# Both seams around an MLP: weight splits in other places, gating on VectorE alone, and a product that goes through its input tiles outside its banks

## The reference, cut to what matters

```python
x = x + m[2] * rms_norm(y, g_post_mix)                       # seam 1: y is the attention's output
f = channel_mlp(modulate(x, g_pre_mlp, m[3], m[4]), w_in, w_out)
x = x + m[5] * rms_norm(f, g_post_mlp)                       # seam 2
# then the next block: modulate(x, g_pre_mix, ...) and its projections
```

## Time and profile before

| | us |
|---|---|
| median of 3 runs | 2458.89 (2457.56 to 2459.14) |
| the profiled execution | 2459.46 |
| its span in the trace | 2458.1 |
| PE busy | 2296.6 (93%) |
| PEld busy | 2095.1 (85%) |
| DVE busy | 1218.8 (50%) |
| ACT busy | 969.9 (39%) |
| POOL busy | 508.9 (21%) |
| DMA, mean over the span | 140 GB/s |

### The profile page before, as it was taken

How to read it: one execution, slowest core, us unless ns; L and a number is a source line. 1 busy time by engine, 2 the same in 40 slices (tenths; PEclk the granted TensorE clock), 3 DMA queues, 4 the chain that set the end, 5 groups by cost and what they waited for, 6 DMA issues and landing times.

```text
span 2458.1 us, 37770 instructions
## 1 busy us (share of the span) xinstructions
PE 2296.6 (93%) x16663; PEld 2095.1 (85%) x16663; DVE 1218.8 (50%) x1517; ACT 969.9 (39%) x1153; POOL 508.9 (21%) x453
## 2 busy tenths in 40 slices
PE   6999899989999999899999899979999979888998
PEld 6999889869999999568999777867888868667997
DVE  5645566556546544456555456352223264544434
ACT  3433444444434333344443345333322334444442
POOL 2112344412112111221220110011211310220220
PEclk8999999999999999799999999989999989899999
DMA  6554443455555554796545110122323323113551
GB/s 246 172 178 166 140 136 123 133 191 172 180 181 177 183 180 157 261 309 239 185 168 187 53 35 18 43 95 86 103 93 96 103 81 103 52 52 103 187 178 64
DMA packets 205246, 344.72 MB, mean 140 GB/s; under 512 B 8846, under 2 KB 69499, under 8 KB 205083
## 3 DMA queue, kind: packets, MB, share of 16 engines
q1 hardware_dynamic: 205082, 342.31, 41.7%
HBM read 341.24 MB, written 1.05 MB: 139 GB/s over the span
## 4 chain that ended last, share of the span: by engine, by line
PE 80%; DVE 9%; POOL 5%; ACT 4%; issue 2%; SPq 0%; DMA 0%; DVEq 0%; POOLq 0%; ACTq 0%
PE PS L467 77%; PE PS L476 3%; DVE WL L453 2%; ACT WH L440 1%; POOL small L1504 1%; DVE rstd L588 1%; DVE XL L635 1%; POOL TMP L1513 1%; POOL small L1502 1%; DVE TMP L1430 0%; DVE XL L1003 0%; DVE al L999 0%; POOL TMP L1514 0%; DVE small L1408 0%; DVE TMP L1435 0%
## 5 line engine op out<-in xcount | busy, mean ns | idle before, releaser
L453 DVE TENSOR_TENSOR WL<-raw,WH 128x2048 fp32r<-128x2048 f32 (+2 forms) x281 | 651.5, 2330 | 721.0 <-ACT WH L440 721.0
L467 PE MATMUL PS<-XH,WH 128*128 128x256 f32 (+1 forms) x2336 | 700.3, 300 | 40.9 <-issue 15.3
L467 PE MATMUL PS<-XL,WH 128*128 128x256 f32 (+1 forms) x2336 | 693.8, 297 | 0.0
L467 PE MATMUL PS<-XH,WL 128*128 128x256 f32 (+1 forms) x2336 | 693.5, 297 | 0.0
L440 ACT ACTIVATE WH<-raw 128x2048 fp32r<-128x2048 f32 (+2 forms) x281 | 518.9, 1859 | 361.5 <-PE PS L467 361.0
L467 PEld LDWEIGHTS PS<-XH,WH 128*128 128x128 f32 x2336 | 452.5, 194 | 57.0 <-issue 18.5
L467 PEld LDWEIGHTS PS<-XL,WH 128*128 128x128 f32 x2336 | 453.5, 194 | 10.0
L467 PEld LDWEIGHTS PS<-XH,WL 128*128 128x128 f32 x2336 | 453.1, 194 | 10.0
L467 PE MATMUL PS<-WH,XH 128*128 128x256 f32 (+2 forms) x944 | 288.3, 305 | 19.1 <-DVE XL L635 8.1
L467 PE MATMUL PS<-WL,XH 128*128 128x256 f32 (+2 forms) x944 | 279.6, 296 | 0.0
L467 PE MATMUL PS<-WH,XL 128*128 128x256 f32 (+2 forms) x944 | 279.4, 296 | 0.0
(11 more groups left out here) (236 smaller groups left out, 2556.8 us busy)
## 6 DMA issues: line engine op xcount, KB each, us to landing
raw<-in_ffn_w_in SPq DMA_DIRECT2D x88, 1024.0 KB, 5.1
raw<-in_w_mod SPq DMA_DIRECT2D x48, 1024.0 KB, 5.3
raw<-in_ffn_w_out SPq DMA_DIRECT2D x40, 1024.0 KB, 4.9
raw<-in_a_w_in SPq DMA_DIRECT2D x36, 1024.0 KB, 4.9
raw<-in_w_mlp_in SPq DMA_DIRECT2D x32, 1024.0 KB, 5.5
raw<-in_w_mlp_out SPq DMA_DIRECT2D x32, 1024.0 KB, 5.0
raw<-in_gla_w_in SPq DMA_DIRECT2D x12, 1024.0 KB, 5.0
raw<-in_attn_w_qkv SPq DMA_DIRECT2D x6, 1024.0 KB, 5.1
```

Source lines behind the costliest of these rows:

```text
L453: dve.e.tensor_tensor(self.WL[j % NRAW][:, 0:nk * nn], self.raw[j % NRAW][:, 0:nk * nn], wh.bitcast(F32), ALU.subtract).then_inc(*self.lo. ...
L467: return self.pe.e.matmul(out, l, r, start=start, stop=stop, skip_group_check=skip)
```

## The change

- The bodies of the split loops become `act_part` and `dve_part`, each of which splits one chunk.
- In the seams, ACT splits the next product's first chunk behind the root of "y1" and its second behind the squares of "n1", ahead of that norm's root. Before, both splits stood behind that root. The copy or square of `Y`'s second half for h=0 goes behind the root.
- DVE splits the first chunk behind the gating of h=1 and the second one a place later, both ahead of the reciprocal of "n1" as before, but no longer waiting for ACT's splits behind the root. The modulation's bias moves into the prenorm, behind the step k = 5.
- All four gatings are on DVE; `gated_pool`, `rest_pool` and the signal `res_pool` go. The third chunk's split on DVE goes behind the gating of h=0.
- `pe_halves` takes the input tiles as the outer loop and the banks as the inner one, and its hooks are called once for each h.

```diff
     def act_begin(self, n=1, held=0):
-        act = self.act
         for i in range(n):
             self.act_begun += 1
             while self.act_split < len(self.parted) and self.parted[self.act_split] < self.act_begun + AHEAD - (held if i + 1 == n else 0):
-                q = self.act_split
-                j = self.parted[q]
-                _, nk, nn, _ = self.stream[j]
-                act.wait_ge(self.raws[j % NRAW], j)
-                if q >= NW:
-                    act.wait_ge(self.lin, self.parted[q - NW])
-                act.e.activation(self.WH[q % NW][:, 0:nk * nn], self.raw[j % NRAW][:, 0:nk * nn], ACT.Copy).then_inc(*self.hi.up(j))
-                self.act_split += 1
+                self.act_part()
+
+    def act_part(self):
+
+        act, q = self.act, self.act_split
+        j = self.parted[q]
+        _, nk, nn, _ = self.stream[j]
+        act.wait_ge(self.raws[j % NRAW], j)
+        if q >= NW:
+            act.wait_ge(self.lin, self.parted[q - NW])
+        act.e.activation(self.WH[q % NW][:, 0:nk * nn], self.raw[j % NRAW][:, 0:nk * nn], ACT.Copy).then_inc(*self.hi.up(j))
+        self.act_split += 1
 
...
+    def dve_part(self):
+
+        dve, q = self.dve, self.dve_split
+        j = self.parted[q]
+        _, nk, nn, _ = self.stream[j]
+        dve.wait_ge(self.hi, j)
+        wh = self.WH[q % NW][:, 0:nk * nn]
+        dve.e.tensor_tensor(self.WL[j % NRAW][:, 0:nk * nn], self.raw[j % NRAW][:, 0:nk * nn], wh.bitcast(F32), ALU.subtract).then_inc(*self.lo.up(j))
+        self.dve_split += 1
...
-    def prenorm_dve(self, tag, h, l, sub, XF, free):
+    def prenorm_dve(self, tag, h, l, sub, XF, free, mid=None):
...
+            if mid and k == 5:
+                mid()
...
         blocks = [self.pe_chunk(src[512 * i:512 * i + 512, :], 4, 512, tag) for i in range(2)]
-        next(hooks, None)
         for h in (1, 0):
-            for b in range(4):
-                bank, at = out(h, b)
-                for kt in range(KT):
-                    c, wh, wl = blocks[kt // 4]
+            for kt in range(KT):
+                c, wh, wl = blocks[kt // 4]
+                for b in range(4):
+                    bank, at = out(h, b)
                     pe.wait_ge(self.lo, c)
                     pe.wait_ge(self.xl, (tags[h], kt))
                     if kt == 0:
                         self.pe_bank(bank)
                     o = slice(b * 128, b * 128 + 128)
                     m = self.mm3(self.PS[:, bank, at:at + 256], (wh[:, kt % 4, o], wl[:, kt % 4, o]), (self.XH[h][:, kt, :], self.XL[h][:, kt, :]), kt == 0, kt == KT - 1)
-                if b == 3:
-                    m.then_inc(*self.lin.up((name, h)))
-                    if h == 0:
-                        for c, _, _ in blocks:
-                            self.lin.name(c)
-                        self.lin.name(name)
-                next(hooks, None)
+            m.then_inc(*self.lin.up((name, h)))
+            next(hooks, None)
+        for c, _, _ in blocks:
+            self.lin.name(c)
+        self.lin.name(name)
...
-    def gated_pool(self, tag, h, q, l, sub, rms, y):
...
         def rest():
-            yield
-            yield
-            yield
-            yield
             for q in range(2):
                 self.pe_sums(t + "n0", 0, q, SQ, self.sq_act, (t + "n0", q), 6, False)
...
         self.to_y_act((t, 1, 1), 1, 1, self.y_banks(1, 1), ((t, "o", 1), 1), first, True)
         self.act_root(t + "y1", 1, 0)
+        self.act_part()
         self.squares_act(t + "n1", 1, self.tiles(self.TMP[:, 2048:4096]), [[(self.res, (t, 1, q))] for q in range(2)])
+        self.act_part()
+        self.act_root(t + "n1", 1, 4)
         self.to_y_act((t, 1, 0), 1, 0, self.y_banks(1, 0), ((t, "o", 1), 0), first, True)
-        self.act_root(t + "n1", 1, 4)
         self.fill_act(1)
         self.act.wait_ge(self.lin, ((t, "o", 1), 0))
...
-        self.squares_act(t + "n0", 0, self.tiles(self.nSQ[0]), [[(self.res_pool, (t, 0, 0))], [(self.res, (t, 0, 1))]])
+        self.squares_act(t + "n0", 0, self.tiles(self.nSQ[0]), [[(self.res, (t, 0, q))] for q in range(2)])
...
         self.dve_invert(t + "y1", 1)
         for q in range(2):
             self.gated_dve(t, 1, q, l, sub, t + "y1", self.y_made(first, (t, q, 1)))
+        self.dve_part()
         if not first:
             self.to_y_dve((t, 1, 0), 1, 0, self.y_banks(1, 0), ((t, "o", 1), 0), before(1, 0))
-        self.dve_mods.send(6)
+        self.dve_part()
         self.dve_invert(t + "n1", 1)
-        self.prenorm_dve(t + "n1", 1, *self.next_norm(l, sub), self.tiles(self.nXF[1]), [(self.lin, ((t, "o", 1), 0))])
+        self.prenorm_dve(t + "n1", 1, *self.next_norm(l, sub), self.tiles(self.nXF[1]), [(self.lin, ((t, "o", 1), 0))], lambda: self.dve_mods.send(6))
 
     def rest_dve(self, t, first, l, sub):
         self.dve_invert(t + "y0", 0)
-        self.gated_dve(t, 0, 1, l, sub, t + "y0", self.y_made(first, (t, 1, 0)))
+        for q in range(2):
+            self.gated_dve(t, 0, q, l, sub, t + "y0", self.y_made(first, (t, q, 0)))
+        self.dve_begin(2, 1)
         self.dve_invert(t + "n0", 0)
-        self.dve.wait_ge(self.res_pool, (t, 0, 0))
         self.prenorm_dve(t + "n0", 0, *self.next_norm(l, sub), self.tiles(self.nXF[0]), [])
...
-    def rest_pool(self, t, first, l, sub):
-        self.gated_pool(t, 0, 0, l, sub, t + "y0", self.y_made(first, (t, 0, 0)))
...
-                self.dve_begin(2, 1 if l == 0 and grp + i == 0 else 0)
                 if l == 0 and grp + i == 0:
                     self.rest_dve("grid", True, 0, 0)
+                else:
+                    self.dve_begin(2)
...
-        self.dve_begin(2, 1)
         self.rest_dve("mlp0", False, 0, 1)
```

More of the change, by code:

```diff
@@ L145 @@
     "lo", "r_dve", "col", "xl", "mean", "diag", "rstd", "gated", "prod", "res", "maxed", "rotated", "emptied", "o_done", "v_step", "y_dve", "mod",
-    "ones", "sq", "powd", "mul", "hl", "p_step", "norm", "res_pool",
+    "ones", "sq", "powd", "mul", "hl", "p_step", "norm",
 ]
@@ L169, in __init__ @@
         self.ones, self.sq, self.powd, self.mul, self.hl = s["ones"], s["sq"], s["powd"], s["mul"], s["hl"]
-        self.p_step, self.norm, self.res_pool = s["p_step"], s["norm"], s["res_pool"]
+        self.p_step, self.norm = s["p_step"], s["norm"]
         self.ld_x, self.ld_ctx, self.ld_rows, self.ld_ident, self.ld_consts = (s[n] for n in LOADS[:5])
@@ L2006, in gated_dve @@
         dve.e.tensor_tensor(R, R, Y[:, 4 * q:4 * q + 4, :], ALU.add).then_inc(*self.res.up((tag, h, q)))
-    def gated_pool(self, tag, h, q, l, sub, rms, y):
-        pool = self.pool
-        Y4, R = self.Y[:, h, 4 * q:4 * q + 4, :], self.R[:, h, 4 * q:4 * q + 4, :]
-        g, rs = self.MA[:, l, 2 * sub + 1, 4 * q:4 * q + 4, 1 - h], self.rstd[:, 256 * h:256 * h + 256]
-        pool.wait_ge(self.rstd_, rms)
-        pool.wait_ge(*y)
-        pool.wait_ge(self.mod, (l, 6 * sub + 5))
-        pool.wait_ge(self.summed, (rms, 1))
-        pool.e.tensor_tensor(Y4, Y4, rs.unsqueeze(1).to_broadcast([128, 4, 256]), ALU.mult).then_inc(*self.p_step.up((tag, "gate", 1)))
-        pool.wait_ge(self.p_step, (tag, "gate", 1))
-        pool.e.tensor_tensor(Y4, Y4, g.unsqueeze(2).to_broadcast([128, 4, 256]), ALU.mult).then_inc(*self.p_step.up((tag, "gate", 2)))
-        pool.wait_ge(self.p_step, (tag, "gate", 2))
-        pool.e.tensor_tensor(R, R, Y4, ALU.add).then_inc(*self.res_pool.up((tag, h, q)))
     def last_products_pe(self, t, src, xs, tags, first):
@@ L2287, in mlp_pool @@
         HH, HL = (self.HH, self.HL) if l else (self.mHH, self.mHL)
-        if l == 0:
-            self.rest_pool("grid", True, 0, 0)
         u = 0
```

10 lines of the change are left out of this document (1 added, 9 removed).

## The result

| | before | changed |
|---|---|---|
| median of 5 runs each | 2458.89 (2457.56 to 2467.46) | 2443.58 (2437.61 to 2446.88) |
| ratio | | 0.9929, interval 0.9907 to 0.995 |
| the profiled execution | 2459.46 | 2443.58 |
| its span | 2458.1 | 2442.0 |

What follows compares the result with a forecast made beforehand. PE bounds the kernel, four fifths of the chain of waits, with holes and half-clock stretches in two seams. Gains of 8.8 and 7.8 us sum to 16.6, from 2459.46 to 2442.9, or 2442.3 for the median; range 2434 to 2450.

Steps and rivals of the forecast that it cites:

- The reciprocal of "n1": On DVE in both seams: starts 5.9 us earlier in seam 1 and 5.3 us earlier in seam 2.
- `Y`'s work behind the root: On ACT: two 1 us steps end ahead of PE's "y0" sums; no cost, 1 us if that cover went.
- The wait for bank 1: Product of h=1: PE makes three matmuls, then waits some 4.4 us for ACT's copy of bank 1 to `MR`.
- The clock term: Each of four products: 2.3 us charged for lowered clock, from 2.9 mean excess less 0.6 waiting for `XL`; bounds 1.3 to 3.7.
- The gating and the "n0" sums: With gating on DVE, "n0" sums follow h=1 without a hole, in 3.61 us, ending at 1624.6 against 1632.1 in seam 1.
- the move of the third split: On DVE, behind the gating: 2.2 us, ending at 1617.7 in seam 1, hidden behind PE's h=1.
- The product of h=0: 4.13 us to first `XL`, then 13.8 us of matmuls; ends 1642.6 in seam 1 and 2034.2 in seam 2.
- The sum: Both seams together: 16.6 us gained, 8.8 in seam 1 and 7.8 in seam 2; median forecast 2442.3 us.
- a clock kept low by changes of bank: Rival, all four products: bank change every 3 matmuls keeps PE at 1.2 GHz, time 2479; 5 in 100 for slower.
- bank 1 as no hindrance: Rival, h=1: runs at full clock from 1602.8, "n0" sums end 6.2 us earlier a seam, time 2430; 6 in 100.
- a clock that stays up: Rival: clock holds over waits of 4.1 to 4.4 us, down to 2433; 8 in 100 for half or more.
- a gain given back outside the seams: Rival: work behind the seams is held by something other than PE, less than 4.9 us left, 2455 to 2459; 5 in 100.

Runs made afterwards that it cites:

- the last version: Changed kernel with modulation block in bank 5, seam 1's `Y` work ahead of the root, first chunk's weight buffer freed mid h=0: 2421.49 us, ratio 0.9848.

## Why the prediction was right

**The reciprocal of "n1".** Forecast 5.9 and 5.3 us earlier, measured 5.9 and 5.4. The working, from durations and idle places in the earlier trace rows, held.

**`Y`'s work behind the root: "no cost".** Wrong, and the largest miss. The step asked when PE's "y0" sums need its output and forgot that PE's turning matmuls write the bank that this work reads. It charged at most 1 us; it cost 3.2 in seam 1, 1.5 as a wait and 1.6 by the slower sums, both of which reach the copy to `MR` through the root of "y0", for which the third `XH` waits. The 1.5 are shown by moving the work back. The 1.6 stand in four profiles of seven, and that the wait brings them is argued.

**The wait for bank 1.** Forecast: three matmuls, then some 4.4 us to the copy. Measured 4.42 and 4.03, and shown by moving the block to bank 5. The copy was due 12.6 and 12.7 us behind the start of the sums; it came at 12.63 in seam 2 and at 15.80 in seam 1, for the reason above.

**The clock term, 2.3 us a product.** Too large in three of four. From the first matmul behind the wait, over 0.12 us each: h=1 13.54 for 93, an excess of 2.4, and 12.74, 1.6; h=0 1639.41 - 1626.31 = 13.10, 1.6, and 13.09, 1.6. Together 7.1 where 9.2 were charged. The 2.9 us from which I took it was a mean over four products, and one of them, 15.23, pulled it up: the other three alone give 14.17 - 11.52 = 2.65, and less the same 0.6 the term would have been 2.05.

**The gating and the "n0" sums.** Forecast: no hole, 3.61 us. Measured so in both seams. The attribution was too simple. In the changed kernel PE is held up so long by bank 1 that POOL's gating would have been in time as well, once the third split stands behind it. The prediction costed the move of the third split at its own 2.2 us; with early splits it also takes ACT's copy and split out of the way of the reciprocal of "y0", 12.6 us of seams in the comparison of splits alone with and without it. That POOL's blanking in seam 2 costs DVE nothing held: at 1983.92 to 1985.3 it lies beside DVE's prenorm steps, which take the same 1.28 us for three and 0.48 for one as in seam 1.

**The product of h=0.** 4.06 us of wait against the forecast 4.13 and 13.1 against 13.8.

**The sum.** 16.6 us forecast. Take 3.2 for the `Y` work, give 2.1 for the clock and 0.1 for the wait ahead of h=0: 15.6, and the seams measured 15.8. The misses partly cancelled, which is luck; so the agreement of 2443.58 with 2442.3 is better than the reasoning behind it. By seams it was 8.8 and 7.8 against 6.4 and 9.4.

**The rivals.** The first, a clock kept low by changes of bank, is refuted: 0.121 us a matmul in the last version. The Trainium skill ("TensorE: Matmul & The Clock Gate", on psum-queue depth-cycling) speaks of small idles from cycling through banks; these traces show none where the reader of the bank is done. The second, bank 1 as no hindrance, fell with the wait of 4.4 us. Its price of 12.4 us for the missing conflict, worked out beforehand, is near what bank 5 gives in the seams, 12.8, but not for the reason given: it was 6.2 us a seam, and bank 5 gives 8.1 in seam 1, 1.6 of them because the "y0" sums took 2.00 us in that profile and not 3.67, so that h=1 began that much earlier, and 4.7 in seam 2. That the two numbers are so close is luck. By the median it is 8.1. The third, a clock that stays up, fell too: within 1 us behind both waits for `MR` matmuls stood 0.21 us apart (1605.48, 1605.69 and so on; in seam 2 from 1989.37). The fourth, a gain given back outside the seams, didn't come for the changed kernel. The splits alone come near it, with 6.6 us in the seams and 1.2 in the median. But the 6.6 are those of the fastest execution, which is itself 5.4 us below the kernel before's median of that job; whether the others lose it in the seams or outside them no profile shows.

## What to carry to other kernels

A loop order also decides when each bank is touched first. Before banks become the inner loop, look up for every bank who read it last and where that instruction stands in its engine's order: here 24 matmuls of cover became 3. One number (bank 5 for bank 1) gave 12.8 us in the seams, and turning the loops back 5.8; in the medians it was 8.1 and 7.6.

Work that is moved "out of the way" of one wait is still waited for by whoever needs its output or its buffer; list all of these, the matmuls of the side work too. And parts of one change are not to be added up: alone they gave 1.2, 2.0 and 10.1 us, together 15.3, and two of them without the third 21.9.
